# Strassen's seven products for one pair of row blocks in the second mixer's input projection

## What is computed

```
def short_conv_mixer(h, buf, w_in, conv_w, w_out):
    proj = h @ w_in
    bg = proj[..., :D_SC]
    cg = proj[..., D_SC:2 * D_SC]
    xin = proj[..., 2 * D_SC:3 * D_SC]
    z = proj[..., 3 * D_SC:]
    conv, new_buf = causal_dwconv(cg * xin, buf, conv_w)
    y = bg * conv * jax.nn.silu(z)
    return y @ w_out, new_buf
```

## Time and profile before

| | |
|---|---|
| median of 3 runs | 909.77 us (909.43 to 911.10) |
| span of the profiled execution, first to last instruction | 906.4 us |
| instructions | 19336 |
| TensorE clock granted, mean | 0.993 |
| PE busy | 881.7 us (97%) |
| DVE busy | 608.0 us (67%) |
| ACT busy | 403.6 us (45%) |
| POOL busy | 147.1 us (16%) |

### The profile page before, as it was taken

One profiled execution on the slowest core, in us unless ns is written; L12 is line 12 of the kernel. 1 busy time (PEld: TensorE's weight loads), 2 busy tenths in 40 slices (PEclk: granted clock), 3 DMA queues, 4 the chain that ended last, 5 costly groups with the idle time before them and its releaser, 6 DMA issues.

```text
span 906.4 us, 19336 instructions
## 1 busy us (share of the span) xinstructions
PE 881.7 (97%) x7385; PEld 870.2 (96%) x7385; DVE 608.0 (67%) x1039; ACT 403.6 (45%) x757; POOL 147.1 (16%) x95
## 2 busy tenths in 40 slices
PE   5999999999999999999999999999999999999996
PEld 5899999999999999989999999999999999999996
DVE  4579999969996999977575444544454555564533
ACT  6568677546855587643522222222211122253334
POOL 5404621433133404630000000000000000000000
PEclk9999999999999999999999999999999999999999
DMA  7336537644655366513343333333333333222212
GB/s 174 108 103 213 169 94 217 186 121 123 209 145 170 115 172 201 166 33 117 97 140 93 93 93 93 93 93 93 93 93 93 91 87 86 91 86 94 93 44 95
DMA packets 162993, 108.00 MB, mean 119 GB/s; under 512 B 5000, under 2 KB 155152, under 8 KB 162368
## 3 DMA queue, kind: packets, MB, share of 16 engines
q1 hardware_dynamic: 123876, 76.15, 28.7%
q10 hardware_dynamic: 38756, 30.61, 11.0%
q0 software_dynamic: 304, 0.48, 0.3%
HBM read 95.35 MB, written 12.14 MB: 119 GB/s over the span
## 4 chain that ended last, share of the span: by engine, by line
PE 76%; DVE 7%; issue 2%; ACT 2%; DMA 1%; DVEq 0%; POOLq 0%; POOL 0%; ACTq 0%
PE pair L1817 34%; PE bank L1817 20%; PE pair L1877 8%; PE pair L2081 5%; PE bank L2081 5%; DVE acc L1194 1%; PE bank L1970 1%; PE bank L1955 1%; PE bank L1719 1%; PE bank L1987 1%; DVE ybuf L1224 1%; DVE wlo L1064 1%; ACT em L711 1%; DMA abc<-a_rows 1%; DMA sample<-in_state_ssm 0%
## 5 line engine op out<-in xcount | busy, mean ns | idle before, releaser
L527 ACT ACTIVATE whi<-raw 128x1024 fp32r<-128x1024 f32 x136 | 143.7, 1057 | 353.9 <-PE bank L1817 137.3
L1817 PE MATMUL pair<-hhi,whi 128*128 128x260 f32 x1136 | 231.7, 285 | 0.2 <-DVE acc L1194 0.2
L1817 PE MATMUL pair<-hhi,wlo 128*128 128x260 f32 x1136 | 229.2, 283 | 0.0
L1817 PE MATMUL pair<-hlo,whi 128*128 128x260 f32 x1136 | 228.7, 283 | 0.0
L1064 DVE TENSOR_TENSOR wlo<-raw,whi 128x1024 fp32r<-128x1024 f32 x132 | 162.2, 1232 | 24.2 <-ACT whi L527 21.8
L1817 PEld LDWEIGHTS pair<-hhi,whi 128*128 128x128 f32 x1136 | 175.5, 189 | 1.9 <-DVE acc L1194 1.0
L1817 PEld LDWEIGHTS pair<-hlo,whi 128*128 128x128 f32 x1136 | 175.6, 189 | 0.0
L1817 PEld LDWEIGHTS pair<-hhi,wlo 128*128 128x128 f32 x1136 | 175.4, 189 | 0.0
L1817 PE MATMUL bank<-hhi,whi 128*128 128x260 f32 x512 | 103.1, 282 | 0.9 <-ACT sqs L512 0.9
L1817 PE MATMUL bank<-hhi,wlo 128*128 128x260 f32 x512 | 103.2, 283 | 0.0
L1817 PE MATMUL bank<-hlo,whi 128*128 128x260 f32 x512 | 103.0, 283 | 0.0
(11 more groups left out here) (256 smaller groups left out, 1306.7 us busy)
## 6 DMA issues: line engine op xcount, KB each, us to landing
raw<-in_sc_w_in SPq DMA_DIRECT2D x64, 512.0 KB, 4.0
raw<-in_ssd_w_in SPq DMA_DIRECT2D x40, 512.0 KB, 4.1
abc<-a_rows ACTq DMA_DIRECT2D x16, 512.0 KB, 4.2
sample<-in_state_ssm ACTq DMA_DIRECT2D x16, 512.0 KB, 4.4
out_new_ssm_s<-sample ACTq DMA_DIRECT2D x16, 512.0 KB, 4.9
raw<-in_ssd_w_out SPq DMA_DIRECT2D x16, 512.0 KB, 3.8
raw<-in_sc_w_out SPq DMA_DIRECT2D x16, 512.0 KB, 3.5
sample<-bc_rows ACTq DMA_DIRECT2D x4, 1024.0 KB, 6.2
```

Source lines behind the costliest of these rows:

```text
L527: act.activation(whi[:, slot, :], raw[:, slot % RAW, :], ACT.Copy).then_inc(hi_done, 1)
L1817: mm = pe.matmul(b, w[:, slot, k * P:(k + 1) * P], h[:, k, cols], start=(k == 0 and i == 0), stop=(k == KT - 1 and i == 2))
```

## The change

Turn 0 stays as it was. In turns 1 to 15 the chunks z and cg ("Z", "G") are whole, and the pair bg (A11, A12 by halves of the 1024 features) and xin (A21, A22) with the four blocks of h (B11 to B22: halves of features by halves of tokens) is made by seven products of 12 matmuls (Winograd's form): P1 = A11 B11, P2 = A12 B21, P3 = S4 B22, P4 = A22 T4, P5 = S1 T1, P6 = -S2 T2, P7 = S3 T3, with signs put into r2. S1 = A21 + A22, S3 = A11 + A21 and S2, S4 are sums of weights (VectorE, `sums_of`), split like a chunk. T1 to T4 are mixes of h before the rms scale; ScalarE weights x again into `h32` (8 copies), GpSimd makes the mixes (4 operations of 1040 columns), ScalarE and VectorE split them (`mix_high`, `mix_low`), once. P1, P6, P7 and P4 add up in bank 4, P5 and P3 in bank 5, P2 in bank 6; ScalarE copies the sums in between out (`snapshot` s, y, t, u) and VectorE adds the corners. PE's order in a turn is Z, P1, P5, P2, P6, P3, P7, G, P4. The first of the three taps goes to ScalarE (`first_tap1`). `raw` has 4 slots instead of 2, the loops are written out, y's first two rows are split inside the last turn, and the output projection starts with three tiles of chunk 0, then the turned conv tails, three tiles of chunk 1, and the fourth tiles.

```diff
+ORDER = ["Z", "S1", "S2", "S4", "A", "S3", "G", "A22"]
+FORM = {f: i + 1 for i, f in enumerate(ORDER)}
+SUM = {"S1": 1, "S3": 2, "S2": 3, "S4": 4}
+STEP = {what: i + 1 for i, what in enumerate(["Z", "P1", "P5", "P2", "P6", "P3", "P7", "G", "P4"])}
...
+        raw = sb("raw", [P, RAWS, 1024])
...
+        h32 = sample[:, 0:KT * T].rearrange("p (k n) -> p k n", n=T)
+        B11, B12, B21, B22 = (h32[:, i * 4:(i + 1) * 4, n * TH:(n + 1) * TH] for i in range(2) for n in range(2))
+        T3, T2, T1 = (flat[:, 2 * i * T:2 * (i + 1) * T].rearrange("p (k n) -> p k n", n=TH) for i in range(1, 4))
+        T4 = B11
...
+        def form_free(eng, j, f):
+            if f == "G":
+                eng.wait_ge(step_done, 9 * (j - 1) + STEP["Z"])
+            elif f == "A22":
+                eng.wait_ge(step_done, 9 * (j - 1) + STEP["P5"])
+            elif j == 1:
+                eng.wait_ge(proj_done, IN1 + {"Z": 1, "A": 2, "S1": 3, "S2": 3, "S4": 4, "S3": 4}[f])
+            else:
+                eng.wait_ge(step_done, 9 * (j - 2) + STEP[{"Z": "P2", "A": "G", "S1": "P6", "S2": "P3", "S4": "P7", "S3": "P4"}[f]])
...
+            def load_part(j, f):
+                place, part = PLACE[f], {"Z": 3, "G": 1, "A": 0, "A22": 2}[f]
+                if j > 1:
+                    sp.wait_ge(form_lo, 8 * (j - 2) + FORM[f])
+                    sp.sem_inc(turnstile, 1)
+                elif place < RAW:
+                    sp.wait_ge(lo_done, IN1 + place + 3 + SLOT)
+                    sp.sem_inc(turnstile, 1)
...
+            load_part(1, "A22")
+            load_part(1, "A")
+            load_part(1, "Z")
+            load_part(1, "G")
+            for j in range(2, TILES):
+                for f in ("Z", "A", "A22", "G"):
+                    load_part(j, f)
...
+            pool.wait_ge(h32_done, KT)
+            pool.tensor_tensor(T3, B22, B12, ALU.subtract).then_inc(mix_done, 1)
+            pool.wait_ge(mix_done, 1)
+            pool.tensor_tensor(T2, T3, B11, ALU.add).then_inc(mix_done, 1)
+            pool.tensor_tensor(T1, B11, B12, ALU.subtract).then_inc(mix_done, 1)
+            pool.wait_ge(mix_done, 3)
+            pool.tensor_tensor(T4, T2, B21, ALU.subtract).then_inc(mix_done, 1)
...
+                    return
+                form_free(act, j, f)
+                if f in SUM:
+                    act.wait_ge(sum_done, 4 * (j - 1) + SUM[f])
+                else:
+                    act.wait_ge(raw_in[PLACE[f]], raw_turn(PLACE[f], j))
+                act.activation(form_of(whi, j, f), form_src(j, f), ACT.Copy).then_inc(form_hi, 1)
...
+                act.wait_ge(step_done, 9 * (j - 1) + STEP[step])
+                if j > 1:
+                    act.wait_ge(gone, j - 1)
+                act.activation(snap_in[what], bank[b][:, 0:TH], ACT.Copy).then_inc(snap_done, 1)
...
+                    act.wait_ge(c21_done, j)
+                    act.wait_ge(c2_done, j)
+                act.activation(acc[:, 0:CONV1], row[:, 0:CONV1], ACT.Copy, scale=colB[:, c1 + j:c1 + j + 1]).then_inc(tapa_done, 1)
...
+            for b in range(2):
+                act.wait_ge(st_st[b], 16 * 9)
+            act.wait_ge(yr_done, TILES + 1)
+            for k in range(KT):
+                act.activation(h32[:, k, :], xT[:, k, :], ACT.Copy, scale=colB[:, n1 + k:n1 + k + 1]).then_inc(h32_done, 1)
+            form_high(1, "Z")
+            form_high(1, "S1")
+            form_high(1, "S2")
+            act.wait_ge(stat_mm, GROUPS + 1)
+            parts = (sqs[:, 1, 0:TH], bank[6][:, 0:TH]), (sqs[:, 1, TH:T], bank[7][:, 0:TH])
+            logs(parts, D)
+            roots(parts, rs_done, GROUPS + 1)
+            load_table(SILU)
+            mix_high(0)
+            mix_high(1)
+            mix_high(2)
+            mix_high(3)
+            silu_z1(0)
+            first_tap1(0)
+            form_high(1, "S4")
+            form_high(1, "A")
+            form_high(1, "S3")
+            for j in range(1, TILES):
+                form_high(j, "G")
+                silu_z1(j)
+                snapshot(j, "s")
+                snapshot(j, "y")
+                form_high(j, "A22")
+                form_high(j + 1, "Z")
+                snapshot(j, "t")
+                if j == TURNS:
+                    y_high1(0)
+                    y_high1(1)
+                snapshot(j, "u")
+                form_high(j + 1, "S1")
+                form_high(j + 1, "S2")
+                form_high(j + 1, "S4")
+                form_high(j + 1, "A")
+                first_tap1(j)
+                form_high(j + 1, "S3")
+            y_high1(2)
+            y_high1(3)
...
+                dve.wait_ge(form_hi, 8 * (j - 1) + FORM[f])
+                dve.tensor_tensor(form_of(wlo, j, f), form_src(j, f), form_of(whi, j, f).bitcast(F32), ALU.subtract).then_inc(form_lo, 1)
...
+                dve.wait_ge(raw_in[PLACE["A22"]], raw_turn(PLACE["A22"], j))
...
+                dve.wait_ge(raw_in[PLACE["A"]], raw_turn(PLACE["A"], j))
+                dve.tensor_tensor(sums["S3"], a11, a21, ALU.add).then_inc(sum_done, 1)
+                dve.wait_ge(sum_done, 4 * (j - 1) + SUM["S1"])
+                dve.tensor_tensor(sums["S2"], sums["S1"], a11, ALU.add).then_inc(sum_done, 1)
+                dve.wait_ge(sum_done, 4 * (j - 1) + SUM["S2"])
+                dve.tensor_tensor(sums["S4"], sums["S2"], a12, ALU.add).then_inc(sum_done, 1)
...
+                cache_row(0)
+                mix_low(0)
+                dve.wait_ge(proj_done, IN1 + 3)
+                dve.wait_ge(cg_free, 2)
+                dve.tensor_tensor(row[:, PRE1:PRE1 + TH], bank[4][:, 0:TH], u[:, 0:TH], ALU.mult)
+                dve.tensor_tensor(row[:, PRE1 + TH:PRE1 + SEQ], bank[5][:, 0:SEQ - TH], u[:, TH:SEQ], ALU.mult)
+                dve.tensor_tensor(dec[:, :, PRE1], bank[5][:, SEQ - TH:TH], u[:, SEQ:T], ALU.mult).then_inc(xin_free, 1)
+                mix_low(1)
+                mix_low(2)
+                weigh_silu(0)
+                conv1(0)
+                mix_low(3)
+                dve.wait_ge(proj_done, IN1 + 4)
+                yt = y_tile1(0)
+                dve.tensor_tensor(yt[:, 0:TH], bank[6][:, 0:TH], c2[:, 0:TH], ALU.mult)
+                dve.tensor_tensor(yt[:, TH:T], bank[7][:, 0:TH], c2[:, TH:T], ALU.mult).then_inc(bg_free, 1)
+                form_low(1, "S4")
...
+            def corner11(j):
+                dve.wait_ge(step_done, 9 * (j - 1) + STEP["P2"])
+                dve.wait_ge(snap_done, 4 * (j - 1) + SNAP["s"])
+                dve.tensor_tensor(bg[:, 0:TH], bank[6][:, 0:TH], snap_in["s"], ALU.add).then_inc(c11_done, 1)
...
+            def corner22(j):
+                dve.wait_ge(snap_done, 4 * (j - 1) + SNAP["u"])
+                dve.tensor_tensor(xin2, snap_in["u"], snap_in["y"], ALU.add).then_inc(c22_done, 1)
...
+                dve.wait_ge(step_done, 9 * (j - 1) + STEP["Z"])
+                dve.wait_ge(sl_done, j)
+                dve.tensor_tensor(zr[:, 0:TH], bank[0][:, 0:TH], r1[:, 0:TH], ALU.mult)
+                dve.tensor_tensor(zr[:, TH:T], bank[1][:, 0:TH], r1[:, TH:T], ALU.mult).then_inc(zr_done, 1)
+                form_low(j, "G")
+                dve.wait_ge(sl_done, j + 1)
+                dve.tensor_tensor(c2, th[:, :], r1, ALU.mult).then_inc(slr_done, 1)
+                form_low(j, "A22")
+                corner11(j)
+                form_low(j + 1, "Z")
+                corner12(j)
+                cache_row(j)
+                sums_of(j + 1)
+                corner22(j)
+                if j == TURNS:
+                    y_low1(0)
+                    y_low1(1)
+                form_low(j + 1, "S1")
+                form_low(j + 1, "S2")
+                form_low(j + 1, "S4")
+                dve.wait_ge(step_done, 9 * (j - 1) + STEP["G"])
+                dve.wait_ge(c22_done, j)
+                dve.tensor_tensor(u[:, TH:T], bank[3][:, 0:TH], r2[:, TH:T], ALU.mult).then_inc(cg_free, 1)
+                dve.tensor_tensor(u[:, 0:TH], bank[2][:, 0:TH], r2[:, 0:TH], ALU.mult).then_inc(cg_free, 1)
+                dve.wait_ge(cg_free, 2 * j + 1)
+                dve.tensor_tensor(row[:, PRE1 + TH:PRE1 + SEQ], xin2[:, 0:SEQ - TH], u[:, TH:SEQ], ALU.mult)
+                dve.tensor_tensor(dec[:, :, PRE1], xin2[:, SEQ - TH:TH], u[:, SEQ:T], ALU.mult)
+                form_low(j + 1, "A")
+                dve.wait_ge(step_done, 9 * (j - 1) + STEP["P4"])
+                dve.wait_ge(cg_free, 2 * j + 2)
+                dve.tensor_tensor(row[:, PRE1:PRE1 + TH], bank[4][:, 0:TH], u[:, 0:TH], ALU.mult).then_inc(c21_done, 1)
+                conv1(j)
+                dve.wait_ge(c11_done, j)
+                dve.wait_ge(c12_done, j)
+                dve.tensor_tensor(y_tile1(j), bg[:, :], c2, ALU.mult).then_inc(bg_free, 1)
+                form_low(j + 1, "S3")
+            dve.wait_ge(sd_done, TILES + 1)
+            dve.wait_ge(t2_done, TILES)
+            sums_of(1)
+            form_low(1, "Z")
+            form_low(1, "S1")
```

(103 more changed lines are left out.)

353 lines of the change are left out of this document (220 added, 133 removed).

## The result

The changed kernel takes **912.94 us** (median of 7 runs, 910.66 to 916.28) against 909.77 (909.43 to 911.19, 7 runs) before: a ratio of 1.004, with an interval of 1.0024 to 1.0057. It is slower by a third of a per cent, where 906.6 and "faster" were forecast. On a second chip the same pair gave 912.61 and 910.55, a ratio of 1.0026 [1.0011, 1.0042].

A forecast was written before the change was run, and what follows sets the result against it. The prediction took the second mixer's input projection as pure TensorE, so only fewer matmuls shorten it. Its terms, -21.6 + 12.3 + 1.6 + 4.5 = -3.2 us, gave 906.6 us, range 898 to 913.

The forecast's parts named there:

- Matmuls removed: Turns 1 to 15: 12 fewer matmuls each, 180 x 0.1201 = 21.6 us off, at an unchanged price in one bank.
- rival (c): Product matmuls cost more in one bank: 2.5 ns each undo the gain, 10 ns give 919 us; chance 0.04.
- VectorE in a turn: Steady turns: VectorE works 17.7 of 21.62 us, ScalarE 9.6; both fit, so no TensorE wait, cost 0.
- rival (b): In the turns VectorE becomes the pace; a turn near 22.5 us would give 920 us; chance 0.13.
- the sign: Expected evidence in the turns if the forecast is right: VectorE busy 17 to 18 us a turn.
- The start: Before turn 1's products: store, copies and high parts delay the logarithm, then mixes delay P1; cost 12.3 us, bounds 11.3 and 13.3.
- P1 is later still: Turn 1: after the bg delay, mixes and VectorE's low parts hold P1 until low A at 472.2 us, instead of 459.9.
- The end: Output projection: TensorE waits 3.8 us instead of 0.9 before chunk 1, plus clock 1.6; +4.5 us, bounds +2 and +6.
- the start's sum: Chain from last store through copies, mixes and VectorE's list to P1 at 472.2 us; cost 12.3 us.
- the clock at the end: Output projection: a TensorE wait of over 2 us brings a low-clock spell costing 1.6 us.
- Rival (d): Start and end cost 2 to 5 us more than reckoned: 908 to 911.5 us, no change that can be told; chance 0.18.
- Rival (a), the hidden front: Start: the h32 chain begins before the norm, leaving at most 4 us of mixes' tail; 897 us; chance 0.13.

The follow-up runs named there:

- mix_vector: The changed kernel with the four mixes on VectorE, behind the first sums, instead of GpSimd: 909.21 us, 0.998 of the kernel before.
- y_first2: The changed kernel with tiles 2 and 3 of y split before the last turn's convolution, not behind it: 907.79 us, 0.9975 of the kernel before.
- all_moved2: The changed kernel with state stores early, mixes on VectorE, logs and roots before turn 1's splits, low A early, y tiles early: 897.03 us, 0.9858 of before.

## Why the prediction was wrong

**Right.** "Matmuls removed": 180 x 120 ns is what went, and one bank costs what two cost (120.4 ns), so rival (c) falls. "VectorE in a turn": 21.65 us a turn and no wait in turns 2 to 15; rival (b) falls. VectorE itself came out lower than reckoned, 16.4 us a turn against 17.7 (the sign asked for 17 to 18): the sum adds up means of records that overlap, such as 0.69 us long and 0.60 apart. "The start": bg's start was put at 454.6 us for a mark at 442.81, which is 11.8 us behind it; it came 11.45 us behind it (458.07 - 446.62). "P1 is later still": that its wait ends on the low part of A, 4.5 us long by the forecast and 4.1 measured, is right too, and so are the first links of the chain, store, copies and logarithm. "The end": the wait before output chunk 1 was reckoned at 3.8 us and is 3.2 (the one that it replaces was 0.59 and not 0.9).

**Wrong: the start's sum, in its last part.** P1 was to come 29.4 us behind the mark and came 33.2 us behind it. GpSimd's mixes themselves took 11.4 us from first to last, as reckoned (4 x 2.86). The step that failed is VectorE's list in that part, and with it the path: the forecast led from the fourth mix over ScalarE's high part and silu to c2, and it was VectorE's own queue that came last. The list begins at c2 (465.8) and leaves out what stands ahead of it in the queue, low Z, S1, S2, r2 and the first low parts of the mixes, as work that the wait for GpSimd covers. That work was costed at nothing with GpSimd itself as its cover. Beside GpSimd the first four cost 11.2 us instead of 3.2, r2 was done only at 467.35, when the last mix was done too (466.8), and then zh, the row and three low parts of mixed forms were still to come before c2 at 473.0. Eight microseconds more, of which 3.8 came through to P1. ScalarE was on time, silu, VectorE's c2, low A:

```profile
468.19 0.64 ACT L1149 ACTIVATE th<-zh 128x520 f32<-128x520 f32 x1 [0.28 <-DVE zh L1875]
473.01 0.69 DVE L1855 TENSOR_TENSOR thx<-th,sqs 128x520 f32<-128x520 f32 x1
478.47 1.22 DVE L1817 TENSOR_TENSOR wlo<-raw,whi 128x1024 fp32r<-128x1024 f32 x1
```

Silu is done 22.2 us behind the mark, where 22.3 was reckoned (465.1 - 442.81), but c2 starts 26.4 us behind it and not 23.0. mix_vector shows the cause by taking GpSimd away: 29.1 us. The same 12.3 us of cost at the start became 16.1.

**Mis-sized in this execution: the clock at the end.** The forecast had 1.6 us for one spell of low clock; the spell behind the wait for chunk 1 cost 3.0 us in this execution and as much in two more, and 1.6 to 1.8 in three others. So the forecast's size is one of the two that occur. With the wait itself the stretch grew by 6.0 us against 4.5, and by 4.3 to 4.5 where the spell was short; y_first2 takes all of it back. In turn 1 the forecast's 1.6 us is nearly right: P1 and the five products behind it took 10.43 us where later turns take 8.67.

```profile
479.84 10.43 PE bank L2408 x72
```

**The sign.** +3.8 and +1.5 us turn -3.2 into +2.1, of the +2.4 that the two changed stretches show; the medians say +3.2 and +2.1. With a short spell at the end the two stretches make +0.7 to +0.9, and then the medians ask for 1 to 2.5 us more, which could be layer 0; no run tells the two apart. Rival (d), start and end dearer by 2 to 5 us, was the right one in kind, with one of its named causes (the longer spell at the low clock) and a dearer one that it did not name, VectorE held up by GpSimd; its price was cut off at 911.5. The +3.8 us of layer 0 in the profiled execution are left out of this sum: what part of them is more than a difference between two executions is open, as said.

**Rival (a), the hidden front,** was judged against the queue order as written. Its price can be had, by order and with the mixes on VectorE: all_moved2 takes 897.0 us.

## What to carry to other kernels

When a change takes work out of a long steady stretch, write out both ends of that stretch queue by queue; here 21.6 us gained in the turns were lost in some 40 us at its edges, and five moves of single operations brought back 15.6. An operation put on GpSimd need not run beside VectorE's: look whether VectorE has two-input work in SBUF at that time, and price that at GpSimd's pace. The longest wait of a trace need not be the one to cure: cutting the 7.5 us one to 5.4 changed nothing, since the queue behind the 4.1 us one set the time.
